# A 31-tap causal convolution re-divided over four engines, with running sums moved into PSUM and four of sixteen summing transfers dropped

## The reference

```python
ya = a_val * jax.nn.sigmoid(a_gate)                    # GLU, 1024 channels
ya = causal_depthwise_conv(ya, conv_a_w, conv_a_b)     # 31 taps, each channel by itself
ya = jax.nn.silu(layer_norm(ya, ln_a_g, ln_a_b))
...
def causal_depthwise_conv(x, w, b):
    k_width = w.shape[0]
    out = lax.conv_general_dilated(
        x, w[:, None, :].astype(x.dtype), window_strides=(1,), padding=[(k_width - 1, 0)],
        dimension_numbers=("NWC", "WIO", "NWC"), feature_group_count=x.shape[-1])
    return out + b
```

## Time and profile before

| | |
|---|---|
| median of 3 runs | 2357.7 us (2353.07 to 2358.66) |
| the profiled execution's own time | 2355.01 us |
| its span | 2353.3 us |
| TensorE (PE) busy | 2330.6 us, 99% |
| VectorE (DVE) busy | 1537.4 us, 65% |
| ScalarE (ACT) busy | 1252.1 us, 53% |
| GpSimd (POOL) busy | 23.2 us, 1% |
| chain that ended last | PE 92%, DVE 4%, ACT 2%, DMA 1% |

### The profile page before, as it was taken

How to read it: one execution, slowest core, us unless ns; L and a number is a source line. 1 busy time by engine, 2 the same in 40 slices (tenths; PEclk the granted TensorE clock), 3 DMA queues, 4 the chain that set the end, 5 groups by cost and what they waited for, 6 DMA issues and landing times.

```text
span 2353.3 us, 39794 instructions
## 1 busy us (share of the span) xinstructions
PE 2330.6 (99%) x13988; PEld 2083.2 (89%) x13988; DVE 1537.4 (65%) x1876; ACT 1252.1 (53%) x1596; POOL 23.2 (1%) x33
## 2 busy tenths in 40 slices
PE   8999999999999999999999999999999999999998
PEld 7899998888888888888888888888888888888887
DVE  7899776555555555678766766765555555556676
ACT  6875655434434445555566666554444444345454
POOL 0011000000000000000000000000000000000000
PEclk9999999999999999999999999999999999999999
DMA  7589675565565555665654555565566556556553
GB/s 248 185 209 216 177 221 172 188 198 186 180 197 192 180 190 192 189 198 176 197 171 153 178 164 178 180 192 188 180 196 196 179 189 203 179 182 202 186 167 120
DMA packets 440781, 439.62 MB, mean 187 GB/s; under 512 B 13568, under 2 KB 438656, under 8 KB 440704
## 3 DMA queue, kind: packets, MB, share of 16 engines
q1 hardware_dynamic: 431968, 429.97, 57.6%
q0 software_dynamic: 8448, 8.39, 2.6%
q10 hardware_dynamic: 288, 0.23, 0.0%
HBM read 428.05 MB, written 2.10 MB: 183 GB/s over the span
## 4 chain that ended last, share of the span: by engine, by line
PE 92%; DVE 4%; ACT 2%; DMA 1%; issue 0%; SPq 0%; DVEq 0%; ACTq 0%
PE ps L464 52%; PE ps L470 27%; PE ps L505 2%; PE ps L507 2%; PE ps L506 2%; PE ps L462 2%; PE ps L469 1%; DVE spl L1296 1%; DMA raw<-in_w_in 1%; PE O L775 1%; ACT spl L833 1%; DVE y L1749 1%; PE O L626 0%; DVE pp L1544 0%; PE Z L600 0%
## 5 line engine op out<-in xcount | busy, mean ns | idle before, releaser
L1296 DVE TENSOR_TENSOR spl<-raw,spl 128x1024 fp32r<-128x1024 f32 x793 | 932.2, 1220 | 583.5 <-ACT spl L833 576.5
L833 ACT ACTIVATE spl<-raw 128x1024 fp32r<-128x1024 f32 (+1 forms) x827 | 832.5, 1054 | 704.2 <-PE ps L470 594.1
L464 PE MATMUL ps<-XA,spl 128*128 128x512 f32 x2816 | 704.8, 392 | 8.1 <-DVE spl L1504 6.8
L464 PE MATMUL ps<-XB,spl 128*128 128x512 f32 x2784 | 711.5, 392 | 0.0
L464 PEld LDWEIGHTS ps<-XA,spl 128*128 128x128 f32 x2816 | 504.9, 189 | 92.7 <-issue 7.3
L464 PEld LDWEIGHTS ps<-XB,spl 128*128 128x128 f32 x2784 | 491.4, 188 | 75.5
L470 PEld LDWEIGHTS ps<-XB,spl 128*128 128x128 f32 x2784 | 394.5, 191 | 39.0
L470 PEld LDWEIGHTS ps<-XA,spl 128*128 128x128 f32 x2816 | 387.1, 191 | 31.4
L470 PE MATMUL ps<-XB,spl 128*128 128x256 f32 x2784 | 402.7, 281 | 0.0
L470 PE MATMUL ps<-XA,spl 128*128 128x256 f32 x2816 | 393.6, 282 | 0.0
L1332 DVE TENSOR_TENSOR tv<-cross,ps 128x512 f32<-128x512 f32 x181 | 123.0, 679 | 13.5 <-ACT cross L833 13.3
(11 more groups left out here) (204 smaller groups left out, 1476.5 us busy)
## 6 DMA issues: line engine op xcount, KB each, us to landing
raw<-in_w_up SPq DMA_DIRECT2D x256, 512.0 KB, 5.0
raw<-in_w_down SPq DMA_DIRECT2D x256, 512.0 KB, 5.2
raw<-in_w_qkv SPq DMA_DIRECT2D x96, 512.0 KB, 4.5
raw<-in_w_gate SPq DMA_DIRECT2D x64, 512.0 KB, 4.5
raw<-in_w_in SPq DMA_DIRECT2D x63, 512.0 KB, 5.0
raw<-in_w_out SPq DMA_DIRECT2D x32, 512.0 KB, 5.0
raw<-in_w_o SPq DMA_DIRECT2D x32, 512.0 KB, 4.7
spl<-raw POOLq DMA_DIRECT2D x16, 512.0 KB, 6.2
```

Of the source, the lines that this page charges most:

```text
L464: pe.matmul(ps[:, b + o, :], w[:, q, 0, c], x[:, kt, :, :], start=start, stop=False)
L833: return act.activation(out, in_, ACT.Copy, scale=scale)
L1296: dve.tensor_tensor(s[:, :, 1, :], raw[:, m % NRAW, :, :], s[:, :, 0, :].bitcast(F32), ALU.subtract).then_inc(lo_ready, 1)
```

## The change

Of the even tile's 31 taps VectorE keeps 19 (`FIRSTS`). For the other 12 ScalarE writes the products `glu * tap` into a ring of five buffers (`prod`, which lies in the unused tensor `rest`), two behind each of the pieces 1 to 6, and GpSimd adds them up in `y`, four (the first time three) behind each summing transfer. VectorE's running sums of both tiles lie in PSUM `Z`, bank 0 for the even and bank 1 for the odd tile; each tile has one running sum. TensorE does 14 instead of 18 taps of the odd tile in the pairs 0 to 2, so VectorE has 17 of them there. `conv_end` copies the odd sum out of PSUM, adds the even one to GpSimd's part, and goes on as before. `SUMMED` loses 57, 65, 73 and 81; their low halves are made by VectorE.

```diff
-TAPS_PE = (18, 18, 18, 12)
+TAPS_PE = (14, 14, 14, 12)
+TAPS_POOL = 12
+FIRSTS = CA - TAPS_POOL
...
+NPROD = 5
+def prod_slot(pair, k):
+    return (pair * TAPS_POOL + k) % NPROD
+def pool_adds(pair, k):
+    return pair * (TAPS_POOL - 1) + max(k, 1)
...
-SUMMED = tuple(range(C_GLU + 17, C_PLE0, 2))
+SUMMED = tuple(k for k in range(C_GLU + 17, C_PLE0, 2) if (k - C_GLU - 17) % 8 < 6)
...
                 pool.wait_ge(neg_ready, n + 1)
                 pool.dma_start(spl[:, m % NSPL, :, 1, :].bitcast(F32), raw[:, m % NRAW, :, :],
                                accum_op=ALU.add).then_inc(lo_summed[m % NSPL], 16)
+                pair, turn = n // 3, n % 3
+                for k in range(max(1, turn * TAPS_POOL // 3), (turn + 1) * TAPS_POOL // 3):
+                    pool.wait_ge(prod_ready, pair * TAPS_POOL + k + 1)
+                    o = y[:, 2 * pair, :]
+                    if k == 1:
+                        pool.tensor_tensor(o, prod[:, prod_slot(pair, 0), :], prod[:, prod_slot(pair, 1), :],
+                                           ALU.add).then_inc(pool_step, 1)
+                    else:
+                        pool.wait_ge(pool_step, pool_adds(pair, k - 1))
+                        pool.tensor_tensor(o, o, prod[:, prod_slot(pair, k), :], ALU.add).then_inc(pool_step, 1)
...
+            def products(pair, turn):
+                act.wait_ge(glu_ready, pair + 1)
+                for k in range(turn * TAPS_POOL // 6, (turn + 1) * TAPS_POOL // 6):
+                    j, g = FIRSTS + k, pair * TAPS_POOL + k
+                    if g >= NPROD:
+                        act.wait_ge(pool_step, pool_adds((g - NPROD) // TAPS_POOL, (g - NPROD) % TAPS_POOL))
+                    copy(prod[:, prod_slot(pair, k), :], glu[:, 2 * pair, j:j + T],
+                         par_col(2 * pair * CA + (CONV_A_W + j))).then_inc(prod_ready, 1)
...
-                first, y2t, second = y[:, bass.ds(pair * 2, 1), :], y2[:, :].unsqueeze(1), y[:, bass.ds(pair * 2 + 1, 1), :]
+                a = pair % 2 * T
+                first, second = Z[:, 0, a:a + T], Z[:, 1, a:a + T]
...
+                for n in range(q * FIRSTS // 8, (q + 1) * FIRSTS // 8):
+                    x, w = glu[:, 2 * pair, n:n + T], par_col(pair * (2 * CA) + (CONV_A_W + n))
...
+                        dve.wait_ge(conv_step, base + n + seconds(n - 1))
+                        r = dve.scalar_tensor_tensor(out=first, in0=x, scalar=w, in1=first, op0=ALU.mult, op1=ALU.add)
...
-                second = y[:, bass.ds(pair * 2 + 1, 1), :]
-                dve.tensor_tensor(second, second, O[:, pair % 2, 0:256].unsqueeze(1), ALU.add).then_inc(conv_taken, 1)
+                a = pair % 2 * T
+                dve.tensor_copy(y[:, 2 * pair + 1, :], Z[:, 1, a:a + T]).then_inc(conv_mixed, 1)
+                dve.wait_ge(pool_step, pool_adds(pair, TAPS_POOL - 1))
+                first = y[:, 2 * pair, :]
+                dve.tensor_tensor(first, first, Z[:, 0, a:a + T], ALU.add).then_inc(conv_mixed, 1)
+                dve.wait_ge(conv_mixed, 2 * pair + 2)
+                second = y[:, 2 * pair + 1, :]
+                dve.tensor_tensor(second, second, O[:, pair % 2, 0:256], ALU.add).then_inc(conv_taken, 1)
```

More of the change, by code:

```diff
@@ L79, in steps_upto @@
 def steps_upto(pair):
-    return sum(2 * CA + 1 - n for n in TAPS_PE[:pair])
+    return sum(FIRSTS + CA - n for n in TAPS_PE[:pair])
+NPROD = 5
[3 more added lines that the diff above has]
+    return pair * (TAPS_POOL - 1) + max(k, 1)
 LAM_STEPS = 17
 OUT_PIECES = ((0, 2), (2, 6), (6, 11), (11, 16))
-SUMMED = tuple(range(C_GLU + 17, C_PLE0, 2))
+SUMMED = tuple(k for k in range(C_GLU + 17, C_PLE0, 2) if (k - C_GLU - 17) % 8 < 6)
 def cuts(m):
@@ L146, in trunk @@
                 nc.sbuf_tensor("xrp", [P, 2, XRP], F32) as xrp, \
-                nc.sbuf_tensor("rest", [P, 8 * 2 * T - 8 * (PAD_A + T) - 2 * XRP], F32), \
+                nc.sbuf_tensor("rest", [P, 8 * 2 * T - 8 * (PAD_A + T) - 2 * XRP], F32) as rest, \
                 nc.sbuf_tensor("rg", [P, 8, 2, T], F32) as rg:
-            pass
+            prod = rest[:, 0:NPROD * T].rearrange("p (k n) -> p k n", k=NPROD)
         XB = sb("XB", [P, NT, 2, T], F32R)
@@ L221, in trunk @@
         conv_step = sem("conv_step")
+        pool_step = sem("pool_step")
+        prod_ready = sem("prod_ready")
+        conv_mixed = sem("conv_mixed")
         ln_sum = sem("ln_sum")
@@ L1154, in glu_pair @@
                     split(C_GLU + NSPL + 8 * c + q)
+                    if 1 <= q < 7:
+                        products(c - 1, q - 1)
                     if c == 1 and q == 4:
@@ L1192, in _ @@
                     split(C_OUTB + 2 * s + q + NSPL)
+                    if 1 <= 2 * s + q < 7:
+                        products(3, 2 * s + q - 1)
                     if s == 7 and q == 0:
@@ L1719, in conv @@
             def conv(pair, q):
-                first, y2t, second = y[:, bass.ds(pair * 2, 1), :], y2[:, :].unsqueeze(1), y[:, bass.ds(pair * 2 + 1, 1), :]
+                a = pair % 2 * T
+                first, second = Z[:, 0, a:a + T], Z[:, 1, a:a + T]
                 base, on_pe = steps_upto(pair), TAPS_PE[pair]
                 def seconds(n):
-                    return n * (CA - on_pe) // (CA + 1)
-                def step(n):
-                    return n + seconds(n)
+                    return n * (CA - on_pe) // FIRSTS
                 if q == 0:
                     dve.wait_ge(glu_ready, pair + 1)
[L1737 to L1743, removed]
-                    if n == 0:
[L1745 to L1749, removed]
-                    else:
-                        r = dve.tensor_tensor(first, first, y2t, ALU.add)
+                for n in range(q * FIRSTS // 8, (q + 1) * FIRSTS // 8):
+                    x, w = glu[:, 2 * pair, n:n + T], par_col(pair * (2 * CA) + (CONV_A_W + n))
+                    if n == 0:
+                        r = dve.tensor_scalar(first, x, w, par_col(pair * 2 + CONV_A_B), ALU.mult, ALU.add)
+                    else:
+                        dve.wait_ge(conv_step, base + n + seconds(n - 1))
+                        r = dve.scalar_tensor_tensor(out=first, in0=x, scalar=w, in1=first, op0=ALU.mult, op1=ALU.add)
                     r.then_inc(conv_step, 1)
@@ L1754, in conv @@
                         j = seconds(n)
-                        x = glu[:, bass.ds(pair * 2 + 1, 1), on_pe + j:on_pe + j + T]
+                        x = glu[:, 2 * pair + 1, on_pe + j:on_pe + j + T]
                         w = par_col(pair * (2 * CA) + (CONV_A_W + CA + on_pe + j))
```

## The result

The changed kernel took 2359.67 us (median of 20 runs, 2354.24 to 2362.79), the kernel before beside it 2354.3 us (20 runs, 2352.81 to 2358.66). The ratio is 1.0018, with a 95% interval of 1.0012 to 1.0024: slower by 0.18%, some 4.2 us, where 4.6 us of gain were forecast. The prediction's range, taken from its own 2357.7, ran from 9.0 us of gain to 2.6 us of loss, so the result lies outside it. As a bare number 2359.67 us lies inside the range of 2348.7 to 2360.3, but only because the 20 runs of the kernel before lie 3.4 us lower than the three that the prediction started from. The profiled execution took 2360.45 us, 5.44 more than that of before.

A forecast was written before the change was run, and what follows sets the result against it. TensorE's own work and a supply line feeding VectorE, meeting at L790, were taken as bounds. The mean came to 255.01 - 4.0 - 1.1 + 0.5 = 250.4, a gain of 4.6 us: 2353.1 us, range 2348.7 to 2360.3.

The forecast's parts named there:

- The step that failed: ScalarE, convolution stretch: 12 us more work, covered by 43.8 us idle except two products, 0.8 us, before chunk 72's rounding.
- the prediction's own signs of being wrong: A new TensorE pause before 222, a summing transfer issued late behind additions, or a mean later than 253.
- VectorE's stretch, -1.1 us: VectorE up to L790: fewer pair 3 steps -5.1, two new low halves +2.3, two `conv_end` +1.7; together -1.1 us.
- the 0.5 us for meeting GpSimd: VectorE's two-SBUF-input instructions ahead of the mean, held up by GpSimd's additions: 0.5 us, bounds 0 and 7.7.
- TensorE*, 5.2 us: TensorE up to L790: twelve taps go, 5.2 us, so it reaches the mean at 247.7.
- Supply line*, -4.8 us: Chunk loads into buffer 3: without four summing transfers beside them, 4.8 us earlier by chunk 71; bounds 0 and 4.8.
- PSUM*, 0: VectorE's running-sum steps: reading and writing PSUM adds 0 to a step of 0.395 us, at most about as much again.
- the rival of slow sums in PSUM: VectorE's steps: same-bank read and write costs 0.27 us a step, mean some 29 us later, about 2387; 8%.
- GpSimd*, 0.7 us an addition: GpSimd's 44 additions take 0.7 us each, bounds 0.30 and 1.29; up to 1.0 us they are through in time.
- The supply line doesn't move: Rival, chunk loads: the 4.8 us becomes 1 or less, gain about 0.8 us, about 2357; 20%.
- GpSimd and VectorE block each other: Rival, pair 3: each addition holds VectorE for its length, mean at 257.6, 2.6 us later than before, 2360.3; 10%.

The follow-up runs named there:

- the best run: The changed kernel with products moved into ScalarE's waits and VectorE's four new low halves moved later: 2349.06 us, 0.9978 of the kernel before.

## Why the prediction was wrong

**The step that failed** is ScalarE's: "It was idle 114 - 70.2 = 43.8 us there, mostly waiting for loads, which covers it. Not covered is what stands between the late load of 71 and the rounding of 72: two products, 0.8 us." The price of two products was right: the instruction behind them starts 0.80 us after the first (204.29 to 205.09). What failed is the claim that idle time covers the rest. The 43.8 us lie in a few long waits, ahead of the late chunk and ahead of the sigmoid. Between those waits ScalarE is itself a link of the supply line: a negative starts a summing transfer, whose end starts the load of the chunk four later, for which ScalarE waits again. Products behind the high halves push back every negative behind them. The wait for the next load gives this back only in part. With products chunk 61 was rounded at 179.80, without them at 173.95; ScalarE's wait for 63 shrank and took up some 4 us, but the load of 65 hangs on the negative of 61, and 65 came at 197.01, not 188.34. Its low half and the sigmoid stand ahead of 66 and 67, and the load of 71 hangs on 67. Chunk 71 came at 218.39 with products, at 211.82 without them, at 211.50 with the same products in the waits. Priced by the runs, the products in their place cost 1.0019 - 0.9987 = 0.0032 or 7.5 us, and 4.9 us by the run that only moves them, where 0.8 stood in the sum.

How far the mean missed its forecast divides at the low half of 72. It started at 222.76 where 215.5 was forecast, so 7.3 of the 7.9 us between the mean's 258.29 and 250.4 were there already. Two of the prediction's own signs of being wrong came true, a new pause of TensorE before 222 and a mean later than 253.

**VectorE's stretch, -1.1 us, came to nothing.** From the low half of 72 to the last sum it took 35.5 us (222.76 to 258.25), as before (219.50 to 254.97); with the 0.5 us for meeting GpSimd, 0.6 less was forecast. The price of a low half was right, what hangs on it was missing. That of 81 waits for a late load (0.32 us in the changed kernel, 1.35 in the run with products moved), and with its own 1.23 us it holds the mean. Moving that one instruction was worth 0.0015, 3.5 us, with what the clock adds. Those of 57, 65 and 73 held the sigmoid, and so ScalarE's next chunk: 11.1 us of waits, before

```profile
ACT tv L1102 <- DVE tv L1682: 7.4, 3, 4.1
```

With these three moved too, chunk 71 came at 213.98, with products as they were; with only that of 81 moved it came at 218.19. Of the difference 3.5 us remain when both are counted from chunk 43. So both feed the delay: moving the products takes 4.9 us off the changed kernel, moving the low halves 5.4, and moving both 9.4.

**What the clock added.** Between the two means TensorE has the same work in all these kernels. By the starts of L790, L818 and L819 it took 264.18 - 255.01 = 9.17 us before and 258.20 - 249.03 = 9.17 in the best run; 268.90 - 258.29 = 10.61 in the changed kernel and 263.28 - 251.65 = 11.63 with products moved. Of the 5.44 us between the profiled executions, 3.28 are the later mean (0.98 of it from ahead of the stretch) and 1.44 the lower clock behind it; the cause of the remaining 0.7 is open, and the runs of one kernel differ by more.

**The other terms held, or nearly.** *TensorE*, 5.2 us: it reaches the mean at 247.6 with products moved and at 249.03 - 1.58 = 247.45 in the best run, forecast 247.7; counted from chunk 43 of each execution this is 4.6 and 5.0 us earlier than before. *Supply line*, -4.8 us: hidden by the step above, and somewhat too large. With products moved chunk 71 comes at 211.50, forecast about 211, and chunk 72's low half at 215.08, forecast 215.5. Part of this closeness is luck: that execution was 0.94 us ahead at chunk 43 (124.40), and counted from there chunk 71 is 3.5 us earlier than before. The four transfers, put back in the best run, cost 5.6 us. In the kernel before, dropped alone, they gave nothing: VectorE's new low halves stood in the way. With these moved, they gave about 2.1 us even without VectorE's savings; the prediction didn't say that this term hangs on where the low halves stand. *PSUM*, 0: VectorE's steps, by source line.

```profile
L1783 DVE SCALAR_TENSOR_TENSOR Z<-glu,params,Z x72: 475/481/490, 143.2 to 253.2; 128x256 f32<-128x256 f32 x72
```

481 ns, against 475 before, and one follows the other by 0.39 us as before: the rival of slow sums in PSUM is out. The Trainium skill (VectorE: DVE Perf Modes, on the TRN2 errata) gives an instruction from PSUM to SBUF a fixed part of 120 cycles where one from SBUF to SBUF has 58; these steps, which read one operand from each and write PSUM, don't show the difference. *GpSimd*, 0.7 us an addition: the median is 742 ns, the mean 1070, longer than forecast, and the run without additions was no faster. GpSimd's additions by line (busy us, mean ns, idle before):

```profile
L474 POOL TENSOR_TENSOR y<-y,rest 128x256 f32<-128x256 f32 x40 | 42.8, 1070 | 7.0 <-ACT rest L861 3.4
```

**The rivals.** "The supply line doesn't move" was the nearest in what the trace shows, but not for its reason: the line moved when ScalarE let it. "GpSimd and VectorE block each other" had the sign, by the wrong mechanism. That the products would be in the way on ScalarE was in none of the cases, so the range was too narrow on that side.

## What to carry to other kernels

Idle time of an engine covers new work only where that work stands in the engine's order. Before work is put down as hidden, look for the rows of the long waits and ask whether the instructions between them feed the thing that is waited for; if they do, place the new work ahead of the wait itself. The same holds for an instruction that waits for a late transfer: put it behind whatever another engine is waiting for, as the one low half here, worth some 3.5 us. And a term that pays only once other instructions are out of the way can be nothing when tried alone: the dropped transfers gave no gain alone (1.0008, 0.9999 to 1.0017) and 0.0024 of gain at the end.

## What the hardware showed unexpectedly

A short pause of TensorE cost more than its length. Granted clock (the first of the last three columns) in the four microseconds at or behind the mean, of the changed kernel, then with products moved, then in the best run:

```profile
258.00:262.00 4.00, 3.71 (x17) 3.53 (x18) 3.66 (x3) 0.13 (x1) 0.00 (x0) 0.57 0.92 323
```

```profile
254.00:258.00 4.00, 4.00 (x23) 4.00 (x23) 2.02 (x2) 2.12 (x2) 0.00 (x0) 0.60 0.40 128
```

```profile
250.00:254.00 4.00, 4.00 (x36) 4.00 (x35) 3.44 (x3) 0.52 (x1) 0.00 (x0) 1.00 0.68 210
```

Ahead of the first TensorE had stood still for 3.01 us, ahead of the second for 4.04, ahead of the third for 1.58. The first two are a mixture of the levels of 1.2 and 2.4 GHz, and the row of the mean, 0.70 us long in the third, took 1.22 in both. The pause before the change (1.9 us, 2.1 for the weight load) had left the clock at 1.00, and so had one of 2.44 us in the run with products and without additions.

GpSimd's additions met VectorE only where VectorE reads two operands from SBUF: in the changed kernel the two sums into `nacc` took 1.69 and 1.34 us with an addition beside them and 0.88 without (212.71, 241.79 and 257.35), and the steps in PSUM stayed at 475 to 490 ns. That is what the Trainium skill (SBUF — State Buffer, on who interferes with whom) says. GpSimd waited there too: its longest additions, up to 2602 ns where the shortest took 722, lay beside such instructions. For the kernel's time it came to no more than the noise: the run with products and without additions was as slow as the changed kernel.
